# Relative-position rows as three products of twelve heads' rows and copied by DMA, small gated-attention products between projections, another order of the last sums

## The reference, cut to what matters

```python
# second block: the bias of dilated attention, four heads in each of three groups
def _group_bias(rel_bias, g, dil):                    # rel_bias: 32 buckets x 12 heads
    qi, kj = np.arange(128)[:, None], np.arange(256)[None, :]
    bucket = _t5_causal_bucket(np.maximum(qi + 128 - kj, 0) * dil)
    tab = rel_bias[:, g * 4:(g + 1) * 4]
    return jnp.transpose(tab[bucket], (2, 0, 1))      # depends on qi - kj alone
# second block: GLA
h = rmsnorm_2(x, ln1[i])
hq, hk, hv, hr, ha, hatt, hgate = _split_cols(h @ w_in[i], SPLIT_SIZES)
log_a = jax.nn.log_sigmoid(ha @ w_a2[i] + b_a[i]) / GLA_TAU     # ha: 512 x 16
o = gla_mixer(hq, hk, hv, log_a)                      # uses the running sum of log_a
# second block: the end
x = x + jax.nn.sigmoid(h3 @ w_pg[i]) * (p[i] @ w_pp[i])
return rmsnorm_2(x, ln_f)                             # needs the sum of x*x over the width
```

## Time and profile before

| | us |
|---|---|
| median of three runs (2000.64, 2001.14, 2004.42) | 2001.14 |
| the profiled execution, its own time | 1998.86 |
| its span in the trace | 1997.1 |
| PE busy | 1938.3 (97%) |
| DVE busy | 949.6 (48%) |
| ACT busy | 775.5 (39%) |
| `rel` products on PE (532.37 to 543.73) | 11.36 |
| `z` and `rt` products on PE | 4.48 and 1.86 |

### The profile page before, as it was taken

How to read it: one execution, slowest core, us unless ns; L and a number is a source line. 1 busy time by engine, 2 the same in 40 slices (tenths; PEclk the granted TensorE clock), 3 DMA queues, 4 the chain that set the end, 5 groups by cost and what they waited for, 6 DMA issues and landing times.

```text
span 1997.1 us, 30886 instructions
## 1 busy us (share of the span) xinstructions
PE 1938.3 (97%) x12878; PEld 1604.8 (80%) x12878; DVE 949.6 (48%) x1497; ACT 775.5 (39%) x1213; POOL 59.5 (3%) x117
## 2 busy tenths in 40 slices
PE   4999998999999999999999999999999999999996
PEld 3887778868788888888699988788888888888885
DVE  5347634556444344445753236543344544344435
ACT  4344544462444123335542252332422442133343
POOL 0000000001230000000001100000000000000000
PEclk9999999999899999999999999999999999999998
DMA  3212110014432223322222222222233323322222
GB/s 145 96 64 95 64 44 5 4 54 130 147 113 95 95 95 98 102 96 95 82 98 103 83 76 98 85 74 75 85 116 109 113 95 101 99 95 95 95 85 85
DMA packets 52284, 178.99 MB, mean 90 GB/s; under 512 B 7115, under 2 KB 7755, under 8 KB 52156
## 3 DMA queue, kind: packets, MB, share of 16 engines
q1 hardware_dynamic: 45184, 161.50, 24.2%
q0 software_dynamic: 5520, 13.04, 2.2%
q10 hardware_dynamic: 1452, 2.56, 0.3%
HBM read 168.41 MB, written 6.55 MB: 88 GB/s over the span
## 4 chain that ended last, share of the span: by engine, by line
PE 95%; DVE 2%; issue 1%; ACT 1%; DMA 1%; ACTq 0%; DVEq 0%
PE bank L646 94%; DMA vec<-in_vecs 1%; DVE ring_lo L1831 1%; PE bank L824 0%; PE bank L710 0%; DVE nr L1845 0%; PE bank L1249 0%; PE bank L796 0%; DVE hf L1867 0%; DVE work_r L1836 0%; DVE bias L2045 0%; ACT work L1325 0%; DVE work L2265 0%; PE bank L1252 0%; DVE x L2267 0%
## 5 line engine op out<-in xcount | busy, mean ns | idle before, releaser
L646 PE MATMUL bank<-work_r,ring_hi 128*128 128x512 f32 x2432 | 759.0, 391 | 1.9 <-ACT work_r L1325 1.3
L1831 DVE TENSOR_TENSOR ring_lo<-ring,ring_hi 128x1024 fp32r<-128x1024 f32 x302 | 367.9, 1224 | 633.7 <-ACT ring_hi L1325 633.3
L646 PEld LDWEIGHTS bank<-work_r,ring_hi 128*128 128x128 f32 x2432 | 457.2, 188 | 100.1 <-issue 3.9
L1325 ACT ACTIVATE ring_hi<-ring 128x1024 fp32r<-128x1024 f32 x302 | 318.6, 1057 | 554.9 <-DMA ring<-in_stream 552.4
L646 PE MATMUL bank<-work_r,ring_lo 128*128 128x512 f32 x1216 | 474.3, 390 | 0.0
L646 PE MATMUL bank<-h_hi,ring_hi 128*128 128x512 f32 x944 | 373.3, 395 | 5.4 <-ACT h_hi L1325 5.4
L646 PE MATMUL bank<-h_hi,ring_lo 128*128 128x512 f32 x944 | 369.3, 391 | 0.0
L646 PEld LDWEIGHTS bank<-work_r,ring_lo 128*128 128x128 f32 x1216 | 228.9, 188 | 47.6 <-issue 0.7
L646 PE MATMUL bank<-h_lo,ring_hi 128*128 128x512 f32 x944 | 231.7, 389 | 0.0
L646 PEld LDWEIGHTS bank<-h_hi,ring_hi 128*128 128x128 f32 x944 | 178.5, 189 | 50.8 <-ACT h_hi L1325 7.0
L646 PEld LDWEIGHTS bank<-h_hi,ring_lo 128*128 128x128 f32 x944 | 178.4, 189 | 38.0 <-issue 1.2
(11 more groups left out here) (216 smaller groups left out, 1567.8 us busy)
## 6 DMA issues: line engine op xcount, KB each, us to landing
ring<-in_stream SPq DMA_DIRECT2D x302, 512.0 KB, 3.3
scratch<-work POOLq DMA_DIRECT2D x12, 192.0 KB, 2.5
x<-in_xT POOLq DMA_DIRECT2D x8, 256.0 KB, 2.9
spill<-x POOLq DMA_DIRECT2D x1, 2048.0 KB, 9.6
work<-x POOLq DMA_DIRECT2D x32, 64.0 KB, 2.1
x<-spill POOLq DMA_DIRECT2D x8, 256.0 KB, 3.0
outT<-hf SPq DMA_DIRECT2D x8, 256.0 KB, 2.1
x<-in_xT ACTq DMA_DIRECT2D x2, 512.0 KB, 6.7
```

The source lines that it names most:

```text
L646: ins = pe.matmul(out, lhsT, rhs, start=start, stop=stop, skip_group_check=True)
L1325: return nc.scalar.activation(out, in_, func, **kw)
L1831: v.tensor_tensor(ring_lo[:, n % RING, :, :], ring[:, n % RING, :, :], ring_hi[:, n % RING, :, :], ALU.subtract).then_inc(sem("split_lo"), 1)
```

## The change

`rel` becomes three jobs, one for each group of the bias: the stationary operand is all twelve columns of `tab`, so that the rows of twelve heads come out on twelve partitions (12x384), and POOL takes four of them from each. ACT copies three banks, each into a tile of its own. POOL writes, for each head, one partition's row of 1536 bytes 128 times (group 0) or 40 times (groups 1 and 2) into `scratch`; it waits for all twelve writes before the 48 reads, and DVE's wait for the writes is on one semaphore. `z`, `rt` and `hq` are put in another order on PE; the code of ACT and DVE for them is not touched. In the last part of block 2 one `add_square` stands behind the last multiply and add.

```diff
-    j += [("hk", i) for i in range(TOGETHER, 4)] + [("z", m) for m in range(RT)] + [("rt",)]
-    j += [("hq", i) for i in range(4)]
+    j += [("hk", 3), ("z", 0), ("z", 1), ("hq", 0), ("z", 2), ("z", 3), ("hq", 1), ("rt",), ("hq", 2), ("hq", 3)]
...
-        j += [("rel", c) for c in range(12)]
+        j += [("rel", g) for g in range(3)]
...
             for c in range(12):
-                pool.wait_ge(*is_drained("rel", c))
-                pool.dma_start(scratch[c, 0:P * RELW].rearrange("(p n) -> p n", n=RELW),
-                               work[:, 40 + c % 4, 0:RELW]).then_inc(sem(f"rel_out{c % 4}"), 16)
+                g = c // 4
+                pool.wait_ge(*is_drained("rel", g))
+                copies = P if g == 0 else 40
+                pool.dma_start(scratch[c, 0:copies * RELW].rearrange("(o p n) -> o p n", o=1, n=RELW),
+                               work[c:c + 1, 40 + g, 0:RELW].unsqueeze(1).broadcast_to([1, copies, RELW])).then_inc(sem("rel_out"), 16)
+            pool.wait_ge(sem("rel_out"), 16 * 12)
...
-            def rel(c):
-
-                out = take("rel", c)
-                single(("rel", c), [(out[:, 0:RELW], tab[0:33, c:c + 1].broadcast_to([33, P]),
-                                     work[0:33, 32 + c // 4, 0:RELW], True, True)])
+            def rel(g):
+
+                out = take("rel", g)
+                single(("rel", g), [(out[0:12, 0:RELW], tab[0:33, 0:12], work[0:33, 32 + g, 0:RELW], True, True)])
...
+            slopes(0)
+            gla_queries(0, 1)
+            slopes(2)
+            gla_queries(1, 2)
             pe.wait_ge(sem("factor"), 1)
             out = take("rt")
             single(("rt",), [(out[:, t:t + 1], factor[:, t * P:(t + 1) * P], ident[:, 0:1], True, True) for t in range(TT)])
-            for i in range(4):
-                project(("hq", i), h2)
-                done_with(1)
+            gla_queries(2, 4)
...
-            def copy_rel(c):
-                split_hi(blocks_to("rel", c))
-                act.wait_ge(*computed("rel", c))
-                if c >= 4:
-                    act.wait_ge(sem(f"rel_out{c % 4}"), 16 * (c // 4))
-                f(work[:, 40 + c % 4, 0:RELW], bank(("rel", c))[:, 0:RELW], ACT.Copy).then_inc(bank_drained[nth("rel", c)], 1)
+            def copy_rel(g):
+                split_hi(blocks_to("rel", g))
+                act.wait_ge(*computed("rel", g))
+                f(work[0:12, 40 + g, 0:RELW], bank(("rel", g))[0:12, 0:RELW], ACT.Copy).then_inc(bank_drained[nth("rel", g)], 1)
...
-                    elif m > 1:
+                    elif 1 < m < DT - 1:
+                        add_square(n0 + 2, m - 2)
+                    elif m == DT:
+                        add_square(n0 + 2, m - 3)
                         add_square(n0 + 2, m - 2)
```

More of the change, by code:

```diff
@@ L589, in _ @@
             for c in range(12):
-                pool.wait_ge(*is_drained("rel", c))
-                pool.dma_start(scratch[c, 0:P * RELW].rearrange("(p n) -> p n", n=RELW),
-                               work[:, 40 + c % 4, 0:RELW]).then_inc(sem(f"rel_out{c % 4}"), 16)
+                g = c // 4
[4 more added lines that the diff above has]
+            pool.wait_ge(sem("rel_out"), 16 * 12)
             for c in range(12):
                 g, hh = divmod(c, 4)
-                pool.wait_ge(sem(f"rel_out{c % 4}"), 16 * (c // 4 + 1))
                 skew = scratch[c, P - 1:P - 1 + P * (RELW - 1)].rearrange("(p n) -> p n", n=RELW - 1)
@@ L1091, in tail @@
                     pe.wait_ge(sem("tab_in"), 16)
-                    for c in range(12):
-                        rel(c)
+                    for g in range(3):
+                        rel(g)
                 for half in range(2):
@@ L1142, in _, with slopes, gla_queries @@
             single(("ha",), [(out[0:16, :], wha_sb[:, k, :], x[:, k, :], k == 0, k == 7) for k in range(8)])
-            for i in range(TOGETHER, 4):
-                project(("hk", i), h2)
-                done_with(1)
+            project(("hk", 3), h2)
+            done_with(1)
+            def slopes(first):
+                for m in range(first, first + 2):
+                    out = take("z", m)
+                    single(("z", m), [(out[:, :], g2_sb[0:16, m * P:(m + 1) * P], work[0:16, HA, :], True, True)])
+            def gla_queries(first, end):
+                for i in range(first, end):
+                    project(("hq", i), h2)
+                    done_with(1)
             pe.wait_ge(*is_drained("ha"))
-            for m in range(RT):
-                out = take("z", m)
-                single(("z", m), [(out[:, :], g2_sb[0:16, m * P:(m + 1) * P], work[0:16, HA, :], True, True)])
+            slopes(0)
+            gla_queries(0, 1)
+            slopes(2)
+            gla_queries(1, 2)
             pe.wait_ge(sem("factor"), 1)
@@ L1607, in tail @@
                 if blk == 1:
-                    for c in range(12):
-                        copy_rel(c)
+                    for g in range(3):
+                        copy_rel(g)
                 act.wait_ge(sem(f"l{n0}"), DT)
@@ L1746, in _ @@
             gla_gates(2, 8)
-            for c in range(8, 12):
-                act.wait_ge(sem(f"rel_out{c % 4}"), 16 * (c // 4 + 1))
             def probs2(i, h, t):
@@ L2241, in tail @@
                     elif blk == 1:
-                        for c in range(4):
-                            dve.wait_ge(sem(f"rel_out{c}"), 48)
+                        dve.wait_ge(sem("rel_out"), 16 * 12)
                     for m in range(DT):
```

## The result

The changed kernel takes 2023.55 us (median of four runs, 2020.48 to 2026.41) against 2000.89 before: a ratio of 1.0111, 95% interval 1.0088 to 1.0133. It is slower by 22.7 us, where 1996 was forecast and 2018 was the upper end of the range. The profiled execution has a span of 2019.8 us for 1997.1.

What follows compares the result with a forecast made beforehand. PE, busy 97% of the span, was taken to bound the kernel. Terms of -11.06 (`rel`), +6.26 (gate) and 0 (end) gave -4.8 from 2001.14, about 1996 us; range 1990 to 2018.

Steps and rivals of the forecast that it cites:

- Part 1 on PE: At `rel`, nine of twelve jobs go (-9.36) and `f1` starts at full clock (-1.71): -11.06 us together.
- The transfers: POOL's `rel` writes, now each out of one partition, were taken to cost PE 0.
- The bound from above: One partition read no faster than one DMA engine, 20.9 GB/s: the `rel` writes last 61 us in all.
- The estimate in the prediction from the page of the Trainium skill: At 27.6 GB/s for partitions 0 to 3, four large writes last 29 us, all twelve up to 47; not used in the sum.
- Rival C: Weights behind `rel`'s one-partition writes starve, PE waits: taken as +18, 2014 us, with 2005 to 2040 around it; chance 0.28.
- drained first or in turn: With 61 us of writes, PE loses about 45 us if they drain before the load, 20 to 30 if packets alternate.
- a source twice as fast: Writes at twice the bound's speed: some 30 us left at the start, 14 at 547, so 6 to 14 lost.
- a slack of 4.0: First weight load behind the writes, issued at 546.98, needs 5.5 of 9.5 us before PE wants its block.
- Part 2: At the gate, DVE's split order delays `hv` 4.55 us after an 8 us PE wait, plus 1.71 clock restart: +6.26.
- D: Rival at the gate: the split order doesn't bite and the spreading gives its 3.4 us: 1987 us, chance 0.10.
- the gain that the spreading alone would give: At the gate, the new order of `z`, `rt` and `hq` on PE alone: -3.4 us if nothing else moves.
- Part 3: At the end, the last sum finishes at the same time, 0.2 us sooner or later: 0.

Runs made afterwards that it cites:

- spread_rel_only: The kernel before with only the `rel` part of `spread`, gate and end as before the change: 1989.59 us against 2001.62, ratio 0.9945.
- spread: The changed kernel with `tab` widened to 32 equal columns a head, rows written from 32 partitions (group 0) or 20 (others): 1996.22 us, ratio 0.9977.

## Why the prediction was wrong

*Part 1 on PE* was right. `f1` begins at 534.35 (forecast 534.29), at a clock of 1.00, nothing else was late, and with a wide source the part is worth -12.0 (`spread_rel_only`, forecast -11.06).

*The transfers* are the step that failed: "I take the lower bound, 0, since the nearest row, the same tiles by the same queue, landed in 2.5 us". That row was nearest in name and line, but its source had 128 partitions, and the width of the source is what the diff changed. Nor were the DMA engines idle beside it: their share was 0.72 to 0.87 from 537.1 on the earlier trace rows. The bound from above was sound: 61 us of copying at one engine's rate, 20.9 GB/s; it was 42.3 us (535.66 to 578.00), of which group 0's part ran at 27.5 GB/s. The estimate in the prediction from the page of the Trainium skill, up to 47 us, came nearest. The term's true size is +24.14 and 2.06 for the clock, +26 instead of 0.

*Rival C* is what happened, with its mechanism and place: the first load behind the writes, issued at 547.75, PE idle on `ring_lo`, POOL's writes landing late. Of its two ways, drained first or in turn, the first was right for this load, as the earlier trace rows had suggested: the writes drained at 577.72, the load landed at 578.98, its block was split 2.3 us later, and PE, which ran out of work at 557.3 (556.5 forecast), waited 24.14. Its price for that way, about 45, came from the 61 us and was too large; the +18 that it was taken as was too small, and the range, which cut C in its middle at 2018, left the result out. Two of C's sums are also off: a source twice as fast, some 30 us from 536 on, leaves 19 us at 547 and not 14, which loses some 15 if drained first and not 6 to 14; and with a slack of 4.0 behind 547 it decides from about 15 us on, not 20. With the earlier trace rows at hand C had deserved more than 0.28: the row that spoke for it (98.0% and 1.5%) was direct, the one against it was of another width.

*Part 2* was right in mechanism and size: wait 7.50 (8 forecast), `hv` +4.92 (+4.55), some 2.1 us more by the half clock behind it (1.71), the copy of `rt` at 19.4 us behind the first `z` (18.8). *D* fell. What the text made too much of is the gain that the spreading alone would give: 3.4 forecast, at most 2.1 seen in the stretch, none in the total.

*Part 3* was right: 0.19 later in the trace, nothing that can be measured.

The sum without the failed step, 1996.3, is what `spread` measured: 1996.22. That it fits to a tenth is luck: the runs of `spread` lie between 1993.85 and 1998.88.

## What to carry to other kernels

When a transfer changes the number of partitions it reads from, price it by a row of the same width or by the bound, never by the same line's old landing time. A slow transfer that nobody waits for still costs when the loads behind it share its engines: count what is queued at once against the slack of the next load, and widen the source or let one be outstanding at a time. And when a job is moved in a list that also sets how far other engines work ahead, follow what each of them now does before it reaches the job that releases the rest.

## What the runs showed of the hardware

Writes out of one partition each gave 27.5 GB/s with 16 busy DMA engines, writes from four neighbours for each of four heads 48 to 58 GB/s in all, and 32 partitions for each head were enough to land 192 KB in 4.5 us. While twelve narrow writes were queued, the weights' queue has no row from 540 to 560; with one outstanding, loads took up to 9.2 and 10.6 us in two profiles. The clock stayed at 1.00 through three `rel` jobs followed at once by `f1`, where it had fallen to 0.50 with twelve. Behind the 24.14 idle us the first ten products ran at 0.50 (4.33 us, 2.27 at full clock).
